# One step of a hybrid decoder layer: the first norm without the expert norm's load, and a reordered router

## The reference, cut to what matters

```
mk, mv   = split(rms_norm(mem, g_mem) @ w_mkv)            # memory keys and values
proj     = rms_norm(x, g_att) @ w_in                      # one projection for all head groups
fox_o, hgrn_o, mem_o = attention, gated recurrence, memory attention (prompt and samples)
h        = x + concat(fox_o, hgrn_o, mem_o) @ w_out
xn       = rms_norm(h, g_ffn)
group    = argmax(xn @ w_rg + b_rg)                       # 1 of 4 groups
top2     = two largest of the group's 8 expert logits     # the choices
gate     = p(group) * softmax(top2 logits)                # the gate values
y        = h + sum over the 2 chosen experts of gate * expert(xn)
```

## Time and profile before

| | us |
|---|---|
| runs, median of 3 | 1893.84 |
| the profiled execution, device time | 1895.96 |
| its span, first to last instruction | 1894.4 |
| PE busy / DVE busy / ACT busy / POOL busy | 1519.7 / 429.6 / 224.1 / 77.2 |
| weights of the experts, share of the chain that ended last (up, down, gate loads) | 18%, 8%, 2% |

### The profile page before, as it was taken

How to read it: one execution, slowest core, us unless ns; L and a number is a source line. 1 busy time by engine, 2 the same in 40 slices (tenths; PEclk the granted TensorE clock), 3 DMA queues, 4 the chain that set the end, 5 groups by cost and what they waited for, 6 DMA issues and landing times.

```text
span 1894.4 us, 23928 instructions
## 1 busy us (share of the span) xinstructions
PE 1519.7 (80%) x9517; PEld 889.2 (47%) x9517; DVE 429.6 (23%) x1126; ACT 224.1 (12%) x502; POOL 77.2 (4%) x141
## 2 busy tenths in 40 slices
PE   5999999999998999999766767577685776857656
PEld 4777777776776666677523132132221322313111
DVE  2206664542133333011300202002020020200201
ACT  3001101002323232011400000000000000000000
POOL 1000000210001222000000000000000000000000
PEclk9999999999999899899888888788888888888888
DMA  7444233431344999644399999999999999999997
GB/s 233 133 134 124 76 134 132 136 118 67 124 159 157 343 376 348 190 133 179 133 405 421 421 421 421 422 422 422 422 422 422 422 422 422 422 422 421 422 421 296
DMA packets 157644, 555.11 MB, mean 293 GB/s; under 512 B 17091, under 2 KB 86788, under 8 KB 108100
## 3 DMA queue, kind: packets, MB, share of 16 engines
q1 hardware_dynamic: 149300, 517.83, 69.5%
q0 software_dynamic: 8272, 36.25, 5.4%
HBM read 545.32 MB, written 8.72 MB: 292 GB/s over the span
## 4 chain that ended last, share of the span: by engine, by line
PE 57%; DMA 33%; DVE 3%; SPq 3%; ACT 2%; issue 1%; POOL 0%; DVEq 0%; ACTq 0%
PE PS L1671 20%; DMA arena<-in_w_up_e_dram 18%; DMA arena<-in_w_down_e_dram 8%; PE PS L2176 7%; PE PS L2123 7%; PE PS L2155 4%; PE PS L2222 4%; PE PS L2213 3%; DMA arena<-in_cache_mem_k_dram 3%; DMA arena<-in_w_gate_e_dram 2%; PE PS L1995 2%; SPq L633 2%; PE PS L1710 1%; PE PS L2055 1%; PE PS L2012 1%
## 5 line engine op out<-in xcount | busy, mean ns | idle before, releaser
L2176 PE MATMUL PS<-arena 128*32 128x512 f32 x2048 | 319.7, 772 | 223.6 <-DMA arena<-in_w_up_e_dram 151.5
L1671 PE MATMUL PS<-arena 128*128 128x288 f32 (+1 forms) x1728 | 444.2, 406 | 3.3 <-DVE arena L1147 1.4
L1671 PEld LDWEIGHTS PS<-arena 128*128 128x128 f32 x1728 | 321.8, 191 | 96.3 <-issue 20.5
L2176 PEld LDWEIGHTS PS<-arena 128*32 128x32 f32 x2048 | 77.8, 137 | 456.6 <-issue 183.4
L2222 PE MATMUL PS<-arena 128*32 128x512 f32 x992 | 150.0, 765 | 76.0 <-DMA arena<-in_w_down_e_dram 76.0
L2123 PE MATMUL PS<-arena 128*128 128x288 f32 x512 | 129.8, 413 | 0.4 <-DVE arena L1435 0.4
L2222 PEld LDWEIGHTS PS<-arena 128*32 128x32 f32 x992 | 36.3, 136 | 183.0 <-issue 95.0
L1588 DVE TENSOR_TENSOR arena<-arena,PS 128x512 f32<-128x512 f32 x8 | 5.5, 687 | 513.0 <-PE PS L2176 513.0
L2123 PEld LDWEIGHTS PS<-arena 128*128 128x128 f32 x512 | 97.1, 192 | 32.0 <-issue 5.5
L2155 PEld LDWEIGHTS PS<-arena 128*128 128x128 f32 x768 | 88.5, 194 | 9.7 <-issue 7.5
L2155 PE MATMUL PS<-arena 128*128 128x128 f32 x768 | 90.9, 279 | 2.0 <-ACT arena L1075 2.0
(11 more groups left out here) (342 smaller groups left out, 1094.7 us busy)
## 6 DMA issues: line engine op xcount, KB each, us to landing
arena<-in_w_gate_e_dram SPq DMA_DIRECT2D x128, 1024.0 KB, 17.9
arena<-in_w_up_e_dram SPq DMA_DIRECT2D x128, 1024.0 KB, 19.8
arena<-in_w_down_e_dram SPq DMA_DIRECT2D x124, 1024.0 KB, 19.0
arena<-in_cache_fox_k_dram SPq DMA_DIRECT2D x64, 384.0 KB, 10.0
arena<-in_cache_fox_v_dram POOLq DMA_DIRECT2D x64, 384.0 KB, 7.3
arena<-in_w_in_dram SPq DMA_DIRECT2D x6, 3072.0 KB, 10.9
arena<-in_w_out_dram SPq DMA_DIRECT2D x8, 2048.0 KB, 8.5
arena<-in_w_in_dram SPq DMA_DIRECT2D x7, 2048.0 KB, 11.0
```

Source lines behind the costliest of these rows:

```text
L1671: last = pe.matmul(PS[0:m, bank, 0:w], wt[:, k, c:c + m], rhs[:, k, :], start=(k == 0), stop=(k == KC - 1))
L2176: last = pe.matmul(PS[x * SLOTS:(x + 1) * SLOTS, which, :], xgT[:, kk, x * SLOTS:(x + 1) * SLOTS], wt[:, k, :], start=(kk == 0), stop=(kk ...
```

## The change

In the first stage `g_ffn_r` moves to the semaphore `wff_in`, which is waited for much later (PE L1782, ACT L938), so PE's wait on `rows_in` falls to 144. ACT waits for five constants only before its first square, and for all 29 before it squares x. DVE takes the second memory tile's sum of squares: a product into `junk_dve` and a reduction, ahead of its work on `cols`.

In the router the choices and `chosen` come ahead of the gate values; `chosen` takes over the buffer `over`, whose zeroing goes; DVE scales the 32 sample rows while PE ranks; the gate values come after `pick_pair(0)`. PE gathers four chunks, not eight, before the first pass, and four ahead of each of quarters 1 to 3.

```diff
-            sp.dma_start(g_ffn_r[:, :].rearrange("p (q k) -> p q k", q=4), g_ffn_norm[0].rearrange("(q p k) -> p q k", q=4, p=P)).then_inc(rows_in, 16)
+            sp.dma_start(g_ffn_r[:, :].rearrange("p (q k) -> p q k", q=4), g_ffn_norm[0].rearrange("(q p k) -> p q k", q=4, p=P)).then_inc(wff_in, 16)
...
         def _(act):
-            act.wait_ge(consts_set, N_CONSTS)
+            act.wait_ge(consts_set, 5)
...
                     src, m, c = NORM[n]
+                    if n == 1:
+                        continue
+                    if n == 2:
+                        act.wait_ge(consts_set, N_CONSTS)
                     act.wait_ge(tok_in[n], 16)
...
             scale_rows(1, P)
-            act.wait_ge(consts_set, N_CONSTS + 1)
-            scale_rows(2, NS)
...
             dve.memset(ssq[:, :], 1.0).then_inc(ssq_clear, 1)
+            dve.wait_ge(tok_in[1], 16)
+            step(dve.tensor_tensor(junk_dve[:, :], NORM[1][0], NORM[1][0], ALU.mult))
+            dve.wait_ge(ssq_done, 1)
+            dve.tensor_reduce(ssq[:, 4:5], junk_dve[:, :], AX.X, ALU.add).then_inc(ssq_done, 1)
 
             dve.wait_ge(cols_filled, 1)
...
             dve.tensor_tensor(dd, m2, m1, ALU.subtract).then_inc(rt_sub, 1)
-            dve.wait_ge(rt_exp, 2)
-            step(dve.tensor_reduce(gsum, ge, AX.X, ALU.add))
...
-            step(dve.tensor_tensor(gb, ga, dd, ALU.mult))
             for n, o in enumerate((o1, o2)):
...
             step(ins)
-            step(dve.tensor_tensor(c1g, choice[:, :, 0, :], bc(ga, NE), ALU.mult))
...
-            chosen = rw[:, :, NE:2 * NE]
             dve.tensor_tensor(chosen, choice[:, :, 0, :], choice[:, :, 1, :], ALU.add).then_inc(moe_prep, 1)
-            dve.memset(over[:, :, :], 0.0)
             step(dve.memset(slot_of[:, :, :], 0.0))
+            dve.wait_ge(consts_set, N_CONSTS + 1)
+            dve.tensor_scalar(by_quarter(h_scaled[0:NS, 2, :]), in_quarters(h_tok[0:NS, 2, :]), rstd[0:NS, 7:8], None, ALU.mult).then_inc(h_scl, 1)
             dve.wait_ge(moe_prep, 2)
...
+            def gate_values():
+                dve.wait_ge(rt_exp, 2)
+                step(dve.tensor_reduce(gsum, ge, AX.X, ALU.add))
+                step(dve.tensor_scalar(ga, dd, 1.0, None, ALU.add))
+                step(dve.tensor_tensor(ga, ga, gsum, ALU.mult))
+                step(dve.reciprocal(ga, ga))
+                step(dve.tensor_tensor(gb, ga, dd, ALU.mult))
+                step(dve.tensor_tensor(c1g, choice[:, :, 0, :], bc(ga, NE), ALU.mult))
+                step(dve.tensor_tensor(rw[:, :, 0:NE], choice[:, :, 1, :], bc(gb, NE), ALU.mult))
+                for t, (t0, w) in enumerate(TILES):
+                    ins = dve.tensor_tensor(gates[0:w, t, :], c1g[0:w, t, :], rw[0:w, t, 0:NE], ALU.add)
+                ins.then_inc(gates_set, 1)
+                dve.wait_ge(gates_set, 1)
...
             pick_pair(0)
+            gate_values()
...
-            pe.wait_ge(rows_in, 160)
+            pe.wait_ge(rows_in, 144)
...
-                            if 1 <= q < 3:
-                                gather(0, range(4 * q + 4, 4 * q + 8))
+                            if q:
+                                gather(0, range(4 * q, 4 * q + 4))
                             pe.wait_ge(xg_drained, q + 1)
...
-            gather(0, range(8))
+            gather(0, range(4))
             pe.wait_ge(slots_set, 2)
```

More of the change, by code:

```diff
@@ L131, in build @@
         junk = view(CAT, D)
+        junk_dve = view(CAT + D, D)
         cat = view(CAT, KC, T)
@@ L232, in build @@
         over = late(3, NE)
+        chosen = over
         n_over = late(2)
@@ L937, in _ @@
             act.wait_ge(ff_filled, 1)
-            act.wait_ge(wff_in, 32)
+            act.wait_ge(wff_in, 48)
             act.activation(ff_strips, PS[:, 2, 0:T], ACT.Copy).then_inc(ff_drained, 1)
@@ L1527, in _ @@
             dve.tensor_tensor(dd, m2, m1, ALU.subtract).then_inc(rt_sub, 1)
-            dve.wait_ge(rt_exp, 2)
-            step(dve.tensor_reduce(gsum, ge, AX.X, ALU.add))
-            step(dve.tensor_scalar(ga, dd, 1.0, None, ALU.add))
-            step(dve.tensor_tensor(ga, ga, gsum, ALU.mult))
-            step(dve.reciprocal(ga, ga))
-            step(dve.tensor_tensor(gb, ga, dd, ALU.mult))
             for n, o in enumerate((o1, o2)):
@@ L1781, in forget_strips @@
             def forget_strips():
-                pe.wait_ge(wff_in, 32)
+                pe.wait_ge(wff_in, 48)
                 pe.wait_ge(ds_used, 3 * HG)
```

## The result

The changed kernel took 1881.03 us, median of 7 runs (1877.08 to 1886.91), beside 1893.19 us for the kernel before (7 runs). The ratio of the means is 0.9946, 95% interval 0.9934 to 0.9959: faster by 7.8 to 12.5 us. The forecast was 1883.5 in 1879 to 1890.

The account below looks back on a forecast made before the run. PE bounds the kernel from 60 us on, the weight stream the experts. First stage 6.0 plus router 5.0 made 11.0, less 0.7 for half clock: 10.3 off the median 1893.84, so 1883.5 us; range with rivals 1879 to 1890.

Parts of the forecast that it names:

- the slower transposes that were feared: First stage: if all 32 transposes go at the slow rate, PE ends 2.3 us later, of which 1.6 is lost.
- The nine loads: First stage: the other nine loads of `rows_in`, taken as in by 13 us, where they cost nothing.
- Rival 3: First stage: DVE's product and reduction become the bound; slower if over 15.7 us together, up to 1906 us; chance 0.04.
- bounds 1.27 to 4.6: Router: DVE's permuted scaling of 32 rows, floor the contiguous 1.27 us, ceiling 4.6; gather gains 3.0 or 1.0.
- the 4.3 of a single profile: Router: the first gather quarter was taken to last 4.3 us, at a mean granted clock of 0.66.
- The allowance of 0.7: Experts: 0.7 us taken off the gain for the half clock reaching some way into the first expert quarter.
- Drain and overflow: Router: PE waits 0.75 us for the quarter's drain; the overflow sum, ready 2.8 after the pick, hides under the quarter.
- Rival 1: Router gives nothing: scaling takes 4.6 us, pick 2.0 late, first expert group at half clock; 1888.2 us; chance 0.12.
- rival 2: First stage keeps its wait, or the 600 to 770 us stretch eats its gain; gain 5.0, 1888.8 us; chance 0.06.
- The worst case of the range: Whole kernel: without a rival's full price, 1.6 us lost in the transposes and 2.0 in the scaling; about 1888 us.

Follow-up runs that it names:

- act_squares: Changed kernel, but ACT squares both memory tiles again and DVE's product and reduction go; 1880.22 us, ratio 0.9936 to the kernel before.
- act_scale: Changed kernel, but ACT instead of DVE scales the 32 sample rows, as before; 1882.62 us, one run.
- gate_first: Changed kernel, but the gate values stand at their old places, ahead of the choices and of `chosen`; 1880.80 us, one run.
- before_again: The kernel before, unchanged, profiled a second time; 1893.92 us, one run.
- first_only: The kernel before with only the first stage's edits, router as before; 1887.65 us, ratio 0.9978 to the kernel before.
- warm: Changed kernel plus 28 unread matmuls ahead of the ranking and 6 ahead of the gather; 1879.62 us, ratio 0.9926 to the kernel before.
- router_only: The kernel before with only the router's edits, first stage as before; 1887.92 us, ratio 0.9976 to the kernel before.

## Why the prediction was right

**First stage: right by its own steps.** Forecast 28.41 to 22.4; measured 22.45. The tile landed at 8.57 (forecast 8.5), the product and the reduction took 2.30 and 2.29 (2.28 each), `cols` came at 13.20 (13.2), and from `cols` to L1671 passed 9.25 for 9.19 before, so the slower transposes that were feared cost nothing. The nine loads were in at 10.05 (by 13). DVE is what is late next, as forecast, and act_squares puts a price on it, about 1 us. The rate taken for both operations, about one element per ns from 1728 elements, held; by the forecast's own terms the reduction comes to 0.457 + 1.76 = 2.22 and not 2.28, which changes nothing that counts. Rival 3 needed 15.7 us for the two and they took 4.6. Over all profiles the gain is 6.2: three unchanged first stages average 28.84, seven changed ones 22.67.

**Router: the sum right, two terms off.** Forecast 5.0. Three old routers average 26.87 from the root to L633 (25.93, 27.39, 27.30), four new ones 21.66 (21.88, 21.05, 21.86, 21.85): 5.2, of which 3.3 lie ahead of the gather and 1.9 behind its start, where the forecast has 3.0 and 2.0. Between the profile of before and that of after alone it is 4.0.
- `chosen` starts 7.71 after the root (916.82 - 909.11), where it was 10.31: 2.6 earlier, forecast 2.46.
- The scaling took 2.06, forecast 2.55, bounds 1.27 to 4.6. It ends 0.5 before the ranks are back, so its length cost nothing. Against the contiguous 1.27 the permuted scaling costs a factor of 1.6 on DVE, not the 2 that was taken over from ACT. The Trainium skill's VectorE: DVE Perf Modes (The perf-mode tier table) gives an f32 `tensor_scalar` of 2048 elements in SBUF 1227 ns; the contiguous row agrees, the permuted 2.06 does not. The Trainium skill's Advanced Engine Details and Errata (SBUF Cachelines) says that a different 16-byte line at each access carries a penalty; this trace agrees, with 2.06 for 1.27.
- The gather starts 3.3 earlier, forecast 3.0. act_scale and gate_first show why it took both edits.
- The first gather quarter is the term that was mis-sized: 5.50 for 4.3. The forecast took the 4.3 of a single profile. The unchanged kernel has 4.32 in that one and 5.46 in before_again and first_only, 5.1 in the mean; the four new routers have 5.50, 4.68, 5.50 and 5.50, 5.3 in the mean. How soon the clock comes back differs from run to run (0.66 and 0.50 in the mean of the quarter for the same kernel), and warm shows what the whole of it is worth. The length stands on both sides of the change and nearly cancels over several profiles; that a sum built on one profile's 4.3 held is in this part luck.
- The allowance of 0.7 stood in the wrong place: it was for the first expert quarter at half clock, which took 3.64 at 1.00, while the gather quarter cost 1.2 more.
- Drain and overflow as forecast: 0.70, and the overflow count runs at 923.42, under the gather quarter.
- Downstream nothing new is late: the DMA share from 935 to 950 is 1.02, and from L633 to the end pass 947.2 for 946.9.

**The absolute marks.** L633 was forecast at 936.4 (rounded; 947.50 - 11.0 is 936.5) and the gather's start at 927.7 (3.0 after 924.7); they came at 930.99 and 921.01. For L633: 7.3 earlier by the sample attention, which was long by chance in the profile of before, 0.95 later by the router and 0.8 later by the other stages. Why that stretch took 177.0 once, no run settles. The forecast took its durations from one execution, and its sum escaped that error because it was made of differences inside two stages and set against the median.

**The rivals.** Rival 1 falls by router_only (the pick isn't late, the expert quarter ran at full clock), rival 2 by first_only, rival 3 by the product's 2.30. In runs the whole is 7.8 to 12.5 us, with the forecast's 10.3 inside. The worst case of the range, 1.6 and 2.0 off the 10.3, is 1887.1 and not 1888; the range is set by rivals 1 and 2 and stays.

## What to carry to other kernels

Where two waits end side by side (a scaling on one engine, a pick on another), each edit alone may give nothing and both together the whole: forecast and test them as a pair. A stage that leaves PE nearly idle (here busy for 0.74 of 8 us) can be paid for in the first work behind it, at half clock; here 34 matmuls that nobody reads bought 2.9 us back in the trace. Before dividing a gain between stages, profile the unchanged kernel a second time: here one untouched stage differed by 6.4 us between two profiles of the same program.

## What the hardware showed that was not expected

- Of the 5.50 us of the first gather quarter nearly half was clock: 2.92 with the clock kept at 1.00. Left alone, the quarter took from 4.32 to 5.46 in four profiles where it starts 15.2 us after the root, and from 4.68 to 5.50 in five where it starts at 11.9: one pair of profiles can be 1.1 us off by this alone.
- A permuted f32 scaling of 2048 elements a partition costs 1.6 times the contiguous one on DVE (2.06 for 1.27). On ACT the permuted scaling takes 2.0 times a contiguous square of the same size (3.83 for 1.91); a contiguous scaling on ACT is not in these traces.
- Handing half of a pair of squares to an idle engine made the stage about 1 us longer: two DVE passes of 2.3 us stand against one ACT pass of 1.91 that makes its sum as it goes.
